# Odd stage: which operand of v's matmuls stays in the array, and where the softmax sums are divided out

## The reference

```
q, k, v = split(rms_norm(x) @ w_qkv)          # 1024, 256 and 256 columns
q, k    = rope(rms_norm(q)), rope(rms_norm(k))
for each of the 16 heads h (k, v of head h // 4):
    p   = softmax(q_h @ k.T * scale)          # 256 x 256
    o_h = p @ v                               # 256 x 64
x = x + concat(o) @ w_out
```

## Time and profile before

| | us |
|---|---|
| median of 3 runs | 1607.78 (1607.54 to 1607.84) |
| the profiled execution | 1607.56 |
| its span in the trace | 1606.2 |
| PE busy over the span | 1586.4 (99%) |
| DVE busy | 1016.7 (63%) |
| ACT busy | 789.5 (49%) |

### The profile page before, as it was taken

The page is one execution under the profiler, slowest core; times in us unless marked ns, Lnnn a source line. Parts: engine busy times, 40 slices in busy tenths (PEclk is TensorE's granted clock), DMA queues, the critical chain, the costliest instruction groups (busy, mean ns, idle before and its releaser), DMA issues.

```text
span 1606.2 us, 19343 instructions
## 1 busy us (share of the span) xinstructions
PE 1586.4 (99%) x7770; PEld 1313.7 (82%) x7770; DVE 1016.7 (63%) x1106; ACT 789.5 (49%) x961; POOL 74.0 (5%) x102
## 2 busy tenths in 40 slices
PE   9999999999999999999999999999999999999999
PEld 7888887888888888898888889977788887678887
DVE  6756677755566555746655476878656457956463
ACT  5545456534354343545543455745444345844342
POOL 1000000100000000100100010010000002000000
PEclk9999999999999999999999999999999999999999
DMA  9555542656565565642565555433455554245551
GB/s 372 180 210 213 190 168 106 239 177 241 181 223 206 194 231 194 219 189 108 193 232 194 214 197 193 163 113 91 154 224 216 204 185 186 88 154 196 200 226 56
DMA packets 88837, 301.99 MB, mean 188 GB/s; under 512 B 26503, under 2 KB 51719, under 8 KB 55978
## 3 DMA queue, kind: packets, MB, share of 16 engines
q1 hardware_dynamic: 88460, 300.17, 51.5%
q10 hardware_dynamic: 288, 0.59, 0.1%
HBM read 287.06 MB, written 1.05 MB: 179 GB/s over the span
## 4 chain that ended last, share of the span: by engine, by line
PE 86%; DVE 8%; ACT 2%; issue 1%; POOL 1%; DMA 1%; SPq 1%; DVEq 0%; ACTq 0%
PE ps L565 83%; DVE wl L2026 2%; PE ps L574 1%; ACT wh L1327 1%; SPq L2883 1%; PE ps L673 1%; DMA raw<-in_w 0%; DVE tmp L2057 0%; POOL st L2795 0%; DVE x L2059 0%; DVE wl L2011 0%; DVE smg L2707 0%; POOL st L2792 0%; DVE xc L2532 0%; DVE scg L2720 0%
## 5 line engine op out<-in xcount | busy, mean ns | idle before, releaser
L2026 DVE TENSOR_TENSOR wl<-raw,wh 128x2048 fp32r<-128x2048 f32 x254 | 571.9, 2288 | 118.5 <-ACT wh L1327 118.4
L565 PE MATMUL ps<-wh,xTh 128*128 128x512 f32 x1408 | 554.2, 394 | 3.7 <-DVE wl L2026 1.1
L565 PE MATMUL ps<-wh,xTl 128*128 128x512 f32 x1408 | 548.7, 390 | 0.0
L565 PE MATMUL ps<-wl,xTh 128*128 128x512 f32 x1408 | 548.2, 389 | 0.0
L1327 ACT ACTIVATE wh<-raw 128x2048 fp32r<-128x2048 f32 x256 | 476.8, 1909 | 7.9 <-PE ps L565 4.8
L565 PEld LDWEIGHTS ps<-wh,xTh 128*128 128x128 f32 x1408 | 264.4, 188 | 62.6 <-issue 2.4
L565 PEld LDWEIGHTS ps<-wh,xTl 128*128 128x128 f32 x1408 | 264.2, 188 | 55.8
L565 PEld LDWEIGHTS ps<-wl,xTh 128*128 128x128 f32 x1408 | 264.5, 188 | 53.1
L2792 POOL TENSOR_SCALAR st<-st 128x1 f32<-128x1 f32 (+2 forms) x46 | 28.6, 622 | 1350.8 <-ACT tmp L1346 791.7
L565 PE MATMUL ps<-xTh,wh 128*128 128x256 f32 x192 | 54.6, 284 | 0.0
L565 PE MATMUL ps<-xTl,wh 128*128 128x256 f32 x192 | 54.3, 283 | 0.0
(11 more groups left out here) (361 smaller groups left out, 2027.3 us busy)
## 6 DMA issues: line engine op xcount, KB each, us to landing
raw<-in_w SPq DMA_DIRECT2D x256, 1024.0 KB, 5.2
gains<-in_rows SPq DMA_DIRECT2D x18, 512.0 KB, 4.1
raw<-in_w SPq DMA_DIRECT2D x8, 512.0 KB, 9.6
hxa<-hsa SPq DMA_DIRECT2D x128, 16.0 KB, 2.3
hxb<-hsb SPq DMA_DIRECT2D x128, 16.0 KB, 2.3
hxc<-hsc SPq DMA_DIRECT2D x128, 16.0 KB, 2.2
hxd<-hsd SPq DMA_DIRECT2D x128, 16.0 KB, 2.1
hxe<-hse SPq DMA_DIRECT2D x128, 16.0 KB, 1.9
```

Source lines behind the costliest of these rows:

```text
L565: return pe.matmul(o, lhs, rhs, start=start, stop=stop, skip_group_check=False)
L2026: TT(wl[:, p % RAW, :], raw[:, p % RAW, :], wh[:, p % RING, :].bitcast(F32), ALU.subtract).then_inc(*lo(p))
```

## The change

The probabilities are no longer divided before the transposes: `turn(i, kk)` waits for the exponentials alone, and what is transposed and copied is the exponentials. `values(i)` now has eight matmuls (t, hh, kk): 128 x 128 of PTg stays in the array and the 64 columns of v stream past, so that the result has 128 queries on the partitions and, in bank 7, 2 x 2 x 64 columns. DVE multiplies it by the reciprocals of the sums (`weighted(i)`) into `gqa_o(i)`, which is a part of pair i's buffer in `r.sc`. PE then transposes that in two blocks (`o_turn(i)`) into the other half of the same bank, and ACT and DVE make the high and low part from there. Per pair one reciprocal of 128 x 4 (`divide(i)`) takes the place of two of 128 x 2 and of the four products. ACT's and DVE's `values` of a pair move one pair later in their orders. The exponentials of pair i now wait for `o_turn(i - 3)` instead of `turn(i - 3, 1)`.

```diff
+        def gqa_o(i):
+            return rooms["odd"].sc[:, i % 3, 0, 0, :]
 # PE
                 def turn(i, kk):
-                    on.wait_ge(made, "gqa", i)
+                    on.wait_ge(exped, "gqa", i, 1)
...
                 def values(i):
                     b = gqa_out(i)
                     clear(b)
                     for kk in range(2):
                         on.wait_ge(copied, "gqa", i, kk)
+                    for t in range(2):
                         for hh in range(2):
-                            m = mm(bank(b)[64 * hh:64 * hh + 64, 0:256], od.vg[:, kk, 64 * (i // 2):64 * (i // 2) + 64],
-                                   r.PT[:, i % 2, kk, hh, :], kk == 0, kk == 1)
+                            n = 128 * t + 64 * hh
+                            for kk in range(2):
+                                m = mm(bank(b)[:, n:n + 64], r.PT[:, i % 2, kk, hh, 128 * t:128 * t + 128],
+                                       od.vg[:, kk, 64 * (i // 2):64 * (i // 2) + 64], kk == 0, kk == 1)
                     m.then_inc(*valued("gqa", i))
                     emptied[b] = [(act_lo, "ogqa", i)]
+                def o_turn(i):
+                    b = gqa_out(i)
+                    on.wait_ge(made, "ogqa", i)
+                    for t in range(2):
+                        m = pe.transpose(bank(b)[:, 256 + 128 * t:384 + 128 * t], gqa_o(i)[:, 128 * t:128 * t + 128], ident[:, :])
+                    m.then_inc(*flipped("ogqa", i))
...
                 q_turn(1, 1)
+                o_turn(0)
+                turn(2, 0)
                 values(1)
-                turn(2, 0)
+                turn(2, 1)
                 out(0, 0)
-                turn(2, 1)
+                o_turn(1)
                 out(0, 1)
                 for i in range(3, 7):
                     scores(i + 1)
...
                     values(i - 1)
                     turn(i, 0)
                     out(i - 2, 0)
+                    o_turn(i - 1)
                     turn(i, 1)
                 out(4, 1)
                 values(6)
                 turn(7, 0)
                 turn(7, 1)
+                o_turn(6)
                 out(5, 0)
                 values(7)
                 out(6, 0)
+                o_turn(7)
                 out(7, 0)
 # ACT
-                            on.wait_ge(turned, "gqa", i - 3, 1)
+                            on.wait_ge(flipped, "ogqa", i - 3)
...
                 def values(i):
-                    on.wait_ge(valued, "gqa", i)
+                    on.wait_ge(flipped, "ogqa", i)
...
-                values(0)
                 turn(1, 1)
                 q_turn(1, 1)
-                values(1)
+                values(0)
                 turn(2, 0)
                 scores(3)
                 for i in range(3, 7):
                     turn(i - 1, 1)
+                    values(i - 2)
                     ring.fill(1, p0 + i + 1)
                     scores(i + 1)
-                    values(i - 1)
                     turn(i, 0)
                 turn(6, 1)
+                values(5)
                 ring.fill(1, p0 + 8)
-                values(6)
                 turn(7, 0)
                 turn(7, 1)
+                values(6)
                 values(7)
 # DVE (scale(i) goes)
+                def sums(i):
+                    return r.sm[:, 12 * (i % 3):12 * (i % 3) + 12].rearrange("p (h n) -> p n h", h=2)
+                def divide(i):
+                    on.wait_ge(exped, "gqa", i, 1)
+                    if i >= 3:
+                        on.wait_ge(made, "ogqa", i - 3)
+                    dve.reciprocal(sums(i)[:, 4:6, :], sums(i)[:, 2:4, :]).then_inc(*made("rc", "gqa", i))
+                def weighted(i):
+                    on.wait_ge(valued, "gqa", i)
+                    on.wait_ge(turned, "gqa", i, 1)
+                    on.wait_ge(made, "rc", "gqa", i)
+                    TT(gqa_o(i).rearrange("p (t h d) -> p t h d", t=2, h=2), bank(gqa_out(i))[:, 0:256].rearrange("p (t h d) -> p t h d", t=2, h=2),
+                       spread(sums(i)[:, 4:6, :], 3, 64), ALU.mult).then_inc(*made("ogqa", i))
...
                 ring.fill(1, p0 + 2)
-                scale(0)
+                divide(0)
                 scores(1)
                 q_rope(1, 0)
                 q_sum(1, 0)
-                scale(1)
+                divide(1)
                 scores(2)
                 q_rope(1, 1)
-                scale(2)
-                values(0)
+                divide(2)
+                weighted(0)
                 q_sum(1, 1)
                 scores(3)
+                values(0)
                 ring.fill(1, p0 + 3)
-                values(1)
+                weighted(1)
                 for i in range(3, 7):
-                    scale(i)
+                    divide(i)
+                    values(i - 2)
                     scores(i + 1)
+                    weighted(i - 1)
                     ring.fill(1, p0 + i + 1)
-                    values(i - 1)
-                scale(7)
+                divide(7)
+                values(5)
+                weighted(6)
+                ring.fill(1, p0 + 8)
                 values(6)
-                ring.fill(1, p0 + 8)
+                weighted(7)
                 values(7)
```

More of the change, by code:

```diff
@@ L1928, in values @@
                 def values(i):
-                    on.wait_ge(valued, "gqa", i)
+                    on.wait_ge(flipped, "ogqa", i)
                     on.wait_ge(multiplied, p0 + 5)
-                    act.activation(xTh[:, i, :, :], bank(gqa_out(i))[:, 0:256].rearrange("p (t n) -> p t n", t=2), ACT.Copy).then_inc(*act_hi("ogqa", i))
+                    act.activation(xTh[:, i, :, :], bank(gqa_out(i))[:, 256:512].rearrange("p (t n) -> p t n", t=2), ACT.Copy).then_inc(*act_hi("ogqa", i))
                 ring.need(p0 + 2)
@@ L2710, in scores @@
                         TT(r.sm[:, a:a + 2], r.sm[:, a:a + 2], gqa_root(2 * i + hh), ALU.mult).then_inc(*peaked("gqa", i, hh))
[L2712 to L2721, removed]
+                def sums(i):
[11 more added lines that the diff above has]
+                       spread(sums(i)[:, 4:6, :], 3, 64), ALU.mult).then_inc(*made("ogqa", i))
                 def values(i):
                     on.wait_ge(act_hi, "ogqa", i)
-                    TT(xTl[:, i, :, :], bank(gqa_out(i))[:, 0:256].rearrange("p (t n) -> p t n", t=2), xTh[:, i, :, :].bitcast(F32), ALU.subtract).then_inc(*act_lo("ogqa", i))
+                    TT(xTl[:, i, :, :], bank(gqa_out(i))[:, 256:512].rearrange("p (t n) -> p t n", t=2), xTh[:, i, :, :].bitcast(F32), ALU.subtract).then_inc(*act_lo("ogqa", i))
                 ring.need(p0 + 2)
```

## The result

The changed kernel takes 1614.84 us (median of 6 runs, 1614.48 to 1615.28) against 1607.81 (1607.54 to 1608.33): slower by 7.0 us, ratio 1.0043 with a 95% interval of 1.0031 to 1.0056. The forecast was 1614.9. The profiled execution took 1614.79 with a span of 1613.5, 7.3 longer than before. The page, part 1, against the earlier trace rows: PE has 7.3 us more, DVE 6.8 less, ACT the same.

The account below looks back on a forecast made before the run. PE, busy 99% of the span, was taken as the bound. 1.5 up to scores(5), 3.6 for values(3) to (7), 1.1 for o_turn(3) to (7) and 1.1 waiting at out(7, 0) gave +7.3 on 1607.56: 1614.9 us, range 1612.2 to 1617.5.

Parts of the forecast that it names:

- Values: PE's values groups: sixteen records in 1.83 us instead of eight in 1.01; +0.72 a pair, +5.8 us for eight.
- o_turn: PE's two added transposes per pair: 0.21 us each time, +1.8 us in all with slower matmuls behind two.
- New waits: PE would newly wait 0.95 us at values(1) for bank 7 and 1.1 us at out(7, 0).
- Level at scores(5): When PE starts scores(5), it would be 1.5 us behind the kernel before.
- Old waits: PE's five waits among the pairs, 2.75 us, put down largely to DVE; about 2.4 us would be regained.
- The balance: Whole stage: added PE work 7.6, old waits regained about 2.4, new waits 2.05; sum +7.3 us.
- Relief in full: Rival: among the pairs all 2.75 us of PE's waits come back, no new ones show; +4.9 us, 1612.4; chance 0.10.
- A wait in each pair: Rival: weighted(i-1) blocks DVE, costing PE about 0.9 us a period for four pairs; +10.9 us, 1618.5; chance 0.08.
- By columns streamed: Rival: PE's values cost goes by streamed columns, about 0.5 us instead of 1.01; -3.0 us, 1604.6; chance 0.04.

Follow-up runs that it names:

- form_only: Kernel before with only the new matmuls in values (exponentials held, v streaming), no o_turn, division where it was: 1611.34 us against 1607.83, ratio 1.0024.
- old_form: Changed kernel with the matmuls of before (v held, 256 columns streaming): 1610.79 us, ratio 1.0019 to the kernel before.
- covered2: Changed kernel, front order as in `covered`, end reordered again with more work between turn(6, 1) and values(6): 1613.21 us, ratio 1.0036 to the kernel before.
- covered: Changed kernel, order only: o_turn(0) ahead of q_turn(1, 1), values(0) earlier on ACT and DVE, end blocks reordered: 1615.77 us, ratio 1.0054 to the kernel before.
- no_division: Kernel before with scale(i), the division by the sums, left out altogether: 1607.46 us against 1607.83, ratio 0.9999.
- stream32: Changed kernel with 32 instead of 64 columns of v streaming in each matmul: 1616.42 us in one run, values group 1.70 us.
- stream128: Changed kernel with 128 instead of 64 columns of v streaming in each matmul: 1614.81 us in one run, values group 1.78 us.

## Why the prediction was right, step by step

**Values: right mechanism, a fifth too dear.** I forecast +0.72 a pair, 5.8 in all, from the even stage's rows of the same form. In the steady loop `form_only` shows 6.66 against 6.09, +0.57. The group takes 1.73 there and not 1.83: both even rows stand behind matmuls of 32 rows, and behind them the group takes the 0.10 again that I had just subtracted on the other side. Behind scores, which have 64 rows, the changed kernel shows 1.83 too (1385.45 to 1387.28). What stands ahead of the second even row in the kernel before, and the group behind scores in the changed one:

```profile
1067.44 0.38 PE L565 MATMUL ps<-selr,trir 32*128 32x512 f32 x2
```

```profile
1385.45 2.00 PE L568 MATMUL ps<-vg,PTg 128*128 128x64 f32 x16
1387.28 0.61 PE L1187 MATMUL ps<-ident,scg 128*128 128x128 f32 x4
```

The other 0.06 of the difference is the transposes behind it, 0.36 instead of 0.42. Pairs 1 and 2 cost more, 0.76 each. Over all eight, `form_only` has 3.58 of distance and 1.38 less of waits than before, 5.0 us together. The bounds of 5.5 to 6.6 did not hold it.

**o_turn: right.** 0.22 in the loop, `old_form` against before 6.30 to 6.09 a period; forecast 0.21.

**New waits: two right in place and size, a third missed.** values(1) 0.87 (0.95 forecast), out(7, 0) 0.93 (1.1). From start to start, as the forecast counted, they are 1.1 (from 1377.56 to 1379.03, less 0.36 for the four transposes) and 1.1 (1.31 from o_turn(7), less 0.21). `old_form` has them alike, and `covered2` removes the second and two thirds of the first by order. The forecast said that values(3) to (7) cost work only; ahead of values(6) and in it PE loses 0.3 us to bank 7, and where `covered` takes out(4, 1) from ahead of it the wait is 1.42.

**Level at scores(5): right.** Scores(1) to scores(5) went from 22.92 to 24.44, +1.52, against the 1.5 taken.

**Old waits: right in sum, wrong in cause.** I wrote that 1.18 is "late because DVE is late", and put the 2.4 us regained down to DVE's relief. The waits kept are 0.46 + 0.35 = 0.81, so 1.94 came back. But `no_division` relieves DVE by more than the change does and regains 0.2, and `form_only` relieves it by nothing and has only 1.4 us of waits left (0.12 at turn(0, 0) by the starts, 0.27, 0.24, 0.35, 0.39). Most of the gaps were filled by PE's own added work: the round over DVE and ACT lasts as long as it does, and a PE with more to do in it waits less. By place: the 0.58 less at scores(3) is values(0); of the 1.18 at turn(3, 1), 0.8 is values(2), as in `form_only`, and the rest is o_turn(2) and ACT's new order; DVE's relief gave the 0.24 at turn(1, 0) alone. The 9.7 of 10 busy on DVE led me astray: the share was high, but what PE waited for last was ACT, as the releasers in the earlier trace rows said for 2.36 of the 2.75 us. The figure came out near because my step-by-step order asked only whether PE still had to wait.

**The balance.** Forecast +7.3 for the stage, measured +6.93. Up to scores(5) it is 1.52 against 1.5. From there to the first transpose of stage f it is 35.17 - 29.76 = 5.41 against 5.8, term by term as the forecast had them: values(3) to (7) 2.9 against 3.6 (the same stretch of `form_only` is 32.62, 2.86 over before); o_turn(3) to (7) and the wait at out(7, 0) together 2.2 as forecast; and the 0.3 at values(6), which it had at nothing. So an error of 0.7 one way and one of 0.3 the other make the 0.4 that is missing. The forecast lies 0.1 from the measured median because it was added to the one profiled execution, 1607.56, which is 0.25 under the median of before: this closeness is luck.

**Rivals.** "Relief in full" fell with `no_division`. "A wait in each pair" did not occur: DVE waits before its products (1.47 before pair 4's), but PE covers that, and no period of the loop shows a wait on PE. "By columns streamed" fell with `stream32` and `stream128`. The Trainium skill's rule in TensorE: Matmul & The Clock Gate, Back-to-back issue gap (about 60 cycles for 1 to 64 columns) is the gap of a matmul without its load; where each matmul brings a new 128-column operand in fp32, the traces have 0.106 to 0.111 us a record.

## What to carry to other kernels

Where each fp32 matmul brings a fresh operand of 128 columns and streams 128 columns or fewer, count records by the columns they hold, not by those they stream: hold the narrow operand (v, 64 columns) and stream the wide one. Before taking work from an engine that is busy 97% of a stretch, look at what the bound engine's waits name as their releaser; if it is another engine, expect little: here the relief brought 0.3 us, at the one lasting wait that named DVE. And when a wait is to be covered by moving a block, look at what that block covered where it stood.

## What the runs showed of the hardware

A record of the new form takes 0.106 us with 32 columns streaming, 0.108 with 64 and 0.111 with 128, all with 128 held, and 0.083 with 96 held. The Trainium skill, TensorE: Matmul & The Clock Gate, section LDWEIGHTS, gives the held columns divided by 1.2 in nanoseconds, by which 128 would be an estimated 107 and 96 an estimated 80; the trace agrees, with 108 and 83. The weight-load records overlap and show 192 and 165 ns each, so their duration is not the price; the distance between groups is. The eight records of before, each with 64 held and 256 streaming, took 1.01 us, 0.126 a record, with the way in and out of the half-width form costing another 0.10 (0.33 instead of 0.23 for the last matmul ahead of them) and 0.06 behind. What sets the 0.126 no run here varies. A group of the new form takes 1.83 instead of 1.73 behind matmuls of 32 or 64 rows, and 1.84 behind a wait (values(1) and (6)).
